# Modulation vectors of a diffusion block on VectorE: multiply-with-sum over transposed weights, streamed through attention

## What is computed

```python
for i in range(2):
    mx = silu(c) @ mod_w[i] + mod_b[i]                 # (6 * 1024,): shift, scale, gate, twice
    sh1, sc1, g1, sh2, sc2, g2 = split(mx, 6)
    h = rmsnorm(x, norm_mix_w[i]) * (1 + sc1) + sh1
    x = x + g1 * mixer_i(h)                            # i = 0: latent attention; i = 1: convolution
    h = rmsnorm(x, norm_ffn_w[i]) * (1 + sc2) + sh2
    x = x + g2 * (routed_experts(h) + shared_expert(h))
out = rmsnorm(x, final_norm_w)
```

## Time and profile before

| | |
|---|---|
| timed runs | 2271.82, 2284.52, 2284.88 us, median 2284.52 |
| profiled execution | 2278.05 us, span 2276.3 us |
| mean granted TensorE clock | 0.932 of full speed |
| DMA | 624 MB, 274 GB/s over the span |

### The profile page before, as it was taken

How to read it: one execution, slowest core, us unless ns; L and a number is a source line. 1 busy time by engine, 2 the same in 40 slices (tenths; PEclk the granted TensorE clock), 3 DMA queues, 4 the chain that set the end, 5 groups by cost and what they waited for, 6 DMA issues and landing times.

```text
span 2276.3 us, 30747 instructions
## 1 busy us (share of the span) xinstructions
PE 1920.7 (84%) x9400; PEld 990.8 (44%) x9401; DVE 829.5 (36%) x1481; ACT 463.6 (20%) x826; POOL 347.8 (15%) x538
## 2 busy tenths in 40 slices
PE   5999999899999888988991798688989889988952
PEld 2455555435444444444440343234444445444521
DVE  2126666504432222222225479425422222222226
ACT  4114444313011111111110355312111101111102
POOL 0000000000111111111105078101011111111122
PEclk8999999998999999999996799798999999999986
DMA  9589000368499999999986500016799999999954
GB/s 371 201 356 346 1 1 1 139 233 336 142 359 415 405 391 399 393 406 394 392 296 240 212 0 1 0 37 260 289 401 403 396 396 407 401 403 390 388 198 170
DMA packets 122815, 624.04 MB, mean 274 GB/s; under 512 B 18048, under 2 KB 19200, under 8 KB 87040
## 3 DMA queue, kind: packets, MB, share of 16 engines
q1 hardware_dynamic: 71776, 498.65, 55.5%
q0 software_dynamic: 26112, 79.72, 9.8%
q10 hardware_dynamic: 24864, 44.84, 5.5%
HBM read 562.34 MB, written 76.28 MB: 281 GB/s over the span
## 4 chain that ended last, share of the span: by engine, by line
PE 62%; DMA 19%; DVE 8%; issue 5%; ACT 3%; POOL 2%; SPq 0%; ACTq 0%; DVEq 0%; POOLq 0%
DMA ring<-in 17%; PE PS L942 10%; PE PS L936 10%; PE PS L1155 5%; PE PS L949 5%; PE PS L963 5%; PE PS L974 4%; PE PS L832 3%; PE PS L1172 3%; PE PS L927 2%; PE PS L861 2%; PE PS L794 2%; POOL work L509 2%; PE PS L917 2%; PE PS L785 2%
## 5 line engine op out<-in xcount | busy, mean ns | idle before, releaser
L942 PE MATMUL PS<-ring,work 128*64 128x256 f32 x3360 | 420.2, 407 | 113.0 <-issue 110.3
L942 PEld LDWEIGHTS PS<-ring,work 128*64 128x64 f32 x3360 | 249.4, 146 | 259.7 <-issue 165.6
L1308 DVE TENSOR_TENSOR work<-work,PS 64x256 f32<-64x256 f32 x105 | 44.4, 423 | 527.9 <-ACT work L583 524.6
L949 PE MATMUL PS<-ring,work 128*64 128x512 f32 x840 | 203.3, 605 | 1.4 <-ACT work L609 0.7
L936 PE MATMUL PS<-ring,work 128*128 128x512 f32 x400 | 177.5, 597 | 15.1 <-issue 12.3
L1313 DVE COPY work<-PS 128x1024 f32<-128x1024 f32 x128 | 156.8, 1225 | 14.7 <-PE PS L974 5.2
L461 POOL COPY col_i<-idx 128x1 int32 (+1 forms) x128 | 23.1, 181 | 839.8 <-PE PS L974 830.4
L467 POOL DMA_INDIRECT work<-h_rows,col_i x128 | 125.5, 981 | 169.0 <-issue 169.0
L974 PE MATMUL PS<-cst,work 128*128 128x128 f32 x1040 | 140.9, 278 | 0.5 <-DMA work<-h_rows,col_i 0.5
L583 ACT ACTIVATE work<-PS 64x256 f32<-64x256 f32 x105 | 39.4, 375 | 489.4 <-PE PS L942 489.4
L974 PEld LDWEIGHTS PS<-cst,work 128*128 128x128 f32 x1040 | 113.4, 141 | 54.0 <-issue 53.0
(11 more groups left out here) (226 smaller groups left out, 2228.5 us busy)
## 6 DMA issues: line engine op xcount, KB each, us to landing
ring<-in SPq DMA_DIRECT2D x156, 2048.0 KB, 11.1
ring<-in SPq DMA_DIRECT2D x130, 1024.0 KB, 12.0
y_rows<-zrow POOLq DMA_DIRECT2D x2, 14336.0 KB, 70.8
y_rows<-work ACTq DMA_DIRECT2D x210, 128.0 KB
ring<-in SPq DMA_DIRECT2D x3, 4096.0 KB, 27.2
y_rows<-work ACTq DMA_DIRECT2D x46, 256.0 KB
ring<-in SPq DMA_DIRECT2D x1, 8192.0 KB, 25.0
ring<-in SPq DMA_DIRECT2D x2, 3072.0 KB, 12.2
```

Of the source, the lines that this page charges most:

```text
L942: last = mm(bank(6)[64 * q:64 * q + 64, 0:F], lhs(c)[:, 0:64], w13(s)[:, q, c, :], start=(c == 0), stop=(c == DC - 1), tile_position=(0, 6 ...
L949: last = mm(bank(4)[64 * q:64 * q + 64, :], actT[par][:, kk, 0:64], w2(s)[:, kk, q * 512:(q + 1) * 512], start=(kk == 0), stop=(kk == 1), ...
```

## The change

- The four chunks that give shift and scale of layer 0's first sub-layer stay on TensorE. The other 10240 columns are computed on VectorE: their weights are transposed on the host, so that 128 of them lie on the partitions with 1024 inputs each, and a block (`mod_block`) is one multiply-with-sum of 128x1024 against SiLU of `c`, which is laid on all partitions by a broadcast load and one SiLU on ScalarE before its first square. Four blocks are a unit, one contiguous load of 2 MB. There are 20 units.
- Units 0 to 4 share one buffer of `ring`, at 12288: 0 and 1 stand on VectorE in front of the key part, 2 to 4 in front of the third latent norm. Units 5 to 13, 36 blocks, stand one block behind the transposes' copy of step n wherever 36n/64, rounded down, goes up. Units 14 to 19 stand three blocks behind each residual of the output projection. They alternate between two buffers at 16384 and 20480. Bias and gain follow in the middle of attention and behind the last block.
- `wq_b` and `wkv_b` are loaded as soon as chunks 0 and 1, and 2, are multiplied, before unit 0. `wo` goes to the start of `ring` and is loaded behind the last up-projection. Router and shared weights of layer 0 wait for the last block.
- The zeros are read from one row of 512 in DRAM instead of `zrow`.
- All weights lie as the SBUF holds them, one contiguous run for each partition. The semaphores of the experts' slots are shared by both layers.

```diff
@@ -42,6 +42,8 @@
+MOD_ROWS = (6 - 2 + 6) * DC
+UNITS = MOD_ROWS // 4
...
@@ -135,12 +137,14 @@
-        mrow = [work[:, n * 512:(n + 1) * 512] for n in range(12)]
+        mrow = [work[:, n * 512:(n + 1) * 512] for n in range(4)]
...
-        wo_sb = ring[:, AW:AW + DC * D].rearrange("p (c f) -> p c f", c=DC)
+        AT = (12288, AW, AW + 4096)
+        mod_tile = [ring[:, at:at + 4 * D].rearrange("p (j d) -> p j d", j=4) for at in AT]
+        wo_sb = ring[:, 0:DC * D].rearrange("p (c f) -> p c f", c=DC)
...
@@ -310,8 +316,17 @@
-        ROW_BANK = [n % 2 for n in range(4)] + [3, 0] * 4 + [(2, 4, 5, 6)[n % 4] for n in range(12)]
-        COL_BANK = [2] * 4 + [3] * 8 + [7] * 12
+        LOADS = [sum(slot_of(u) == n for u in range(E)) for n in range(RING)]
...
+        ROW_BANK = [n % 2 for n in range(4)]
+        COL_BANK = 2
+        EARLY = 5
...
+        ATTN_BLOCKS = 4 * (UNITS - 6 - EARLY)
...
+        def unit_home(u):
+            return (0, u + 1) if u < EARLY else (1 + (u - EARLY) % 2, (u - EARLY) // 2 + 1)
...
@@ -349,15 +363,19 @@
-                if n % 12 >= MODBUF:
-                    sp.wait_ge(modrow_ps, n - MODBUF + 1)
-                j = n % 12
-                sp.dma_start(mw[n % MODBUF], mod_w[n // 12, :, j * 512:(j + 1) * 512].rearrange("(c p) f -> p c f", p=128))\
-                  .then_inc(modw_in[n % MODBUF], 16)
+                sp.dma_start(ring[:, n * DC * 512:(n + 1) * DC * 512], mod_w[n]).then_inc(modw_in[n], 16)
...
+            def load_unit(u):
+                at, n = unit_home(u)
+                if u < EARLY:
+                    sp.wait_ge(modt_used, u)
+                elif u >= EARLY + 2:
+                    sp.wait_ge(modt_used, u - 1)
+                sp.dma_start(mod_tile[at].rearrange("p j d -> p (j d)"), mod_t[u]).then_inc(modt_in[at], 16)
...
-                sp.dma_start(rw_sb, router_w[i].rearrange("(c p) e -> p c e", p=128)).then_inc(rw_in, 16)
+                sp.dma_start(rw_sb.rearrange("p c e -> p (c e)"), router_w[i]).then_inc(rw_in, 16)
...
@@ -408,29 +426,30 @@
+            sp.dma_start(cs_row, c_row.partition_broadcast(128)).then_inc(crow_in, 16)
...
-            sp.dma_start(wqa_sb, wq_a.rearrange("(c p) f -> p c f", p=128)).then_inc(aw_in, 16)
-            sp.dma_start(wkva_sb, wkv_a.rearrange("(c p) f -> p c f", p=128)).then_inc(aw_in, 16)
-            for n in range(MODBUF, 12):
-                load_mod(n)
-            sp.wait_ge(modrow_ps, 12)
-            sp.dma_start(wqb_sb, wq_b.rearrange("(c p) (h f) -> p c h f", p=128, h=H)).then_inc(bw_in, 16)
-            sp.dma_start(wkvb_sb, wkv_b.rearrange("(c p) (h f) -> p c h f", p=128, h=H)).then_inc(bw_in, 16)
+            sp.dma_start(ring[:, AW:AW + DC * (QL + KVW)], w_a).then_inc(aw_in, 16)
+            sp.wait_ge(modrow_ps, 3)
+            sp.dma_start(ring[:, 0:8192], wq_b).then_inc(bw_in, 16)
+            sp.dma_start(ring[:, 8192:12288], wkv_b).then_inc(bw_in, 16)
+            sp.wait_ge(modrow_ps, 4)
+            for u in range(EARLY):
+                load_unit(u)
...
-            sp.dma_start(wo_sb, wo.rearrange("(c p) f -> p c f", p=128)).then_inc(wo_in, 16)
+            for u in range(EARLY, UNITS - 6):
+                load_unit(u)
...
-            for n in range(12, 15):
-                load_mod(n)
+            sp.dma_start(ring[:, 0:DC * D], wo).then_inc(wo_in, 16)
+            for u in range(UNITS - 6, UNITS):
+                load_unit(u)
...
-            for n in range(15, 24):
-                load_mod(n)
-            sp.wait_ge(wo_ps, DC)
+            sp.wait_ge(modt_used, UNITS)
...
-            sp.dma_start(pw1_sb, pw1.rearrange("(c p) f -> p c f", p=128)).then_inc(pw_in, 16)
-            sp.dma_start(pw2_sb, pw2.rearrange("(c p) f -> p c f", p=128)).then_inc(pw2_in, 16)
+            sp.dma_start(pw1_sb.rearrange("p c f -> p (c f)"), pw1).then_inc(pw_in, 16)
+            sp.dma_start(pw2_sb.rearrange("p c f -> p (c f)"), pw2).then_inc(pw2_in, 16)
...
@@ -514,7 +533,7 @@
-                               zrow[:, :].unsqueeze(1).to_broadcast([128, E // 2 + XMAX, 512])).then_inc(zero_out, 16)
+                               zero_d.unsqueeze(1).to_broadcast([128, E // 2 + XMAX, 512])).then_inc(zero_out, 16)
...
@@ -538,9 +557,12 @@
+            a.wait_ge(crow_in, 16)
+            A(cs_row, cs_row, ACT.Silu).then_inc(crow_rdy, 1)
...
-                A(mrow[n % 12], bank(ROW_BANK[n]), ACT.Copy).then_inc(modrow_sb, 1)
+                A(mrow[n], bank(ROW_BANK[n]), ACT.Copy).then_inc(modrow_sb, 1)
...
@@ -716,16 +736,11 @@
-            for n in range(DC + 1):
-                if n < DC:
-                    mod_row(12 + n)
-                if n:
-                    a.wait_ge(wo_ev, n)
-                    square(J_FFN0, n - 1)
+            for n in range(DC):
+                a.wait_ge(wo_ev, n + 1)
+                square(J_FFN0, n)
...
-            for n in range(20, 24):
-                mod_row(n)
...
@@ -831,8 +843,6 @@
-                for n in LATE[LSQ.index(g)] if g in LSQ else []:
-                    mod_chunk(n)
...
@@ -920,7 +926,6 @@
-                mod_chunk(12 + n)
...
@@ -1130,10 +1129,6 @@
-            for n in range(20, 24):
-                mod_chunk(n)
-            for n in range(12, 20):
-                mod_columns(n)
...
@@ -1205,6 +1199,31 @@
+            def mod_block(u, j):
+                at, n = unit_home(u)
+                g, c = u // 2, 4 * (u % 2) + j
+                i, part = (0, 2 + g) if g < 4 else (1, g - 4)
+                if j == 0:
+                    dve.wait_ge(modt_in[at], 16 * n)
+                last = V.scalar_tensor_tensor(mod_tile[at][:, j, :], mod_tile[at][:, j, :], 1.0, cs_row, ALU.mult, ALU.mult,
+                                              accum_out=mod[i][:, part, c, 0:1])
+                if j == 3:
+                    last.then_inc(modt_used, 1)
...
+            def mod_unit(u):
+                for j in range(4):
+                    mod_block(u, j)
...
+            def mod_done(i, units, p0, p1, gains):
+                dve.wait_ge(modt_used, units)
+                link(V.tensor_tensor(mod[i][:, p0:p1, :, 0].rearrange("p s c -> p (s c)"),
+                                     mod[i][:, p0:p1, :, 0].rearrange("p s c -> p (s c)"),
+                                     v("modb", 48 * i + DC * p0, 48 * i + DC * p1), ALU.add))
+                for n, g in gains:
+                    last = V.scalar_tensor_tensor(modA[i][:, n, :, 0], mod[i][:, 3 * n + 1, :, 0], 1.0,
+                                                  v(g, DC * i, DC * i + DC), ALU.add, ALU.mult)
+                last.then_inc(mod_rdy, 1)
...
@@ -1217,7 +1236,10 @@
-            mod_out(0, 4, COL_BANK[0], 0, 2, [(0, "nmix")])
+            mod_out(0, 4, COL_BANK, 0, 2, [(0, "nmix")])
+            dve.wait_ge(crow_rdy, 1)
+            mod_unit(0)
+            mod_unit(1)
...
@@ -1235,6 +1257,9 @@
+                if J == 2:
+                    for u in range(2, EARLY):
+                        mod_unit(u)
...
@@ -1256,7 +1281,6 @@
-            mod_out(0, 12, COL_BANK[4], 2, 6, [(1, "nffn")])
...
@@ -1284,12 +1308,18 @@
-            dve.wait_ge(mod_rdy, 2)
+                for b in range(n * ATTN_BLOCKS // NS, (n + 1) * ATTN_BLOCKS // NS):
+                    mod_block(EARLY + b // 4, b % 4)
+                if n == NS // 2:
+                    mod_done(0, 8, 2, 6, [(1, "nffn")])
...
+                for b in range(3 * n, 3 * n + 3):
+                    mod_block(UNITS - 6 + b // 4, b % 4)
+            mod_done(1, UNITS, 0, 6, [(0, "nmix"), (1, "nffn")])
...
@@ -1360,8 +1390,6 @@
-                if i == 0:
-                    mod_out(1, 24, COL_BANK[12], 0, 6, [(0, "nmix"), (1, "nffn")])
...
@@ -1606,8 +1634,13 @@
-    ins = [feats(a["x"][0]), feats(a["ctx"][0]), vec, constants(), a["mod_w"], a["mla_wq_a"][0], wq_b, wkv_a, wkv_b,
-           a["mla_wo"][0], a["conv_pw1_w"][0], a["conv_pw2_w"][0], a["router_w"], a["router_bias"], exp_w, sh_w]
+    w_a = np.concatenate([on_partitions(a["mla_wq_a"][0], DC), on_partitions(wkv_a, DC)], axis=1)
+    mod_w = np.stack([on_partitions(a["mod_w"][0][:, n * 512:(n + 1) * 512], DC) for n in range(4)])
+    mod_t = np.concatenate([a["mod_w"][0][:, 2 * D:], a["mod_w"][1]], axis=1).T
+    mod_t = mod_t.reshape(UNITS, 4, 128, D).transpose(0, 2, 1, 3).reshape(-1, 128, 4 * D)
+    ins = [feats(a["x"][0]), feats(a["ctx"][0]), vec, constants(), a["c"], np.zeros((1, 512), np.float32), mod_w, mod_t, w_a,
+           on_partitions(wq_b, QL // 128), on_partitions(wkv_b, KVL // 128), on_partitions(a["mla_wo"][0], DC),
+           on_partitions(a["conv_pw1_w"][0], DC), on_partitions(a["conv_pw2_w"][0], DC), on_partitions(a["router_w"], DC), a["router_bias"], exp_w, sh_w]
...
```

50 lines of the change are left out of this document (18 added, 32 removed).

## The result

The changed kernel took 2305.54 us, the median of eight runs (2294.7 to 2325.09); the kernel before, beside it on the same chip, 2283.6. The ratio is 1.0114, with a 95% interval of 1.0069 to 1.0158: slower, by about 1%. The eight times stand in two groups, 2294.7 to 2299.1 and 2312.0 to 2325.1, four in each, with a mean of 2297.4 and of 2318.6. The profiled execution, 2311.96 us, is of the upper one.

A forecast was written before the change was run, and what follows sets the result against it. TensorE, busy 84% of the span, was taken as the bound, so only what ends last counts. Terms +0.5 + 20.0 - 14.8 - 7.1 = -1.4 gave 2276.7 (profiled) or 2283.1 (median); forecast 2280 us, range 2252 to 2312.

The forecast's parts named there:

- Start: Before the down-projections: the broadcast of c and a SiLU delay ScalarE's first square, all serial; loss 2.4 us, bounds 1.0 to 6.
- Early loads: Units 0 to 4 before attention: each load beside the zeros takes 11 us, bounds 7.2 to 14.6; attention starts 0.5 later.
- That rival: Early unit loads starve beside zeros from one DRAM row: 20 us each, attention 28 later, 2308 us; chance 0.18.
- Restart at half clock: At attention's query half, TensorE restarts after some 20 us of idle at the 1.2 GHz level: a loss of 2.35 us.
- Attention: In attention, 36 blocks of 1.35 us on VectorE cost 20.0 us where its chain runs; bounds 0 to 49.
- My own table of steps: Cost of an attention block by step: 1.14 us behind 2, 1.35 behind 3 or 4, 0.64 behind 5 or 6, otherwise nothing.
- The rival of free blocks: VectorE's blocks cost nothing in attention because it idles 110 of 300 us: 2260 us, 2252 with quickest loads; chance 0.17.
- Output projection and norm: After attention, up to the score transposes: removed TensorE chunks gain 14.8 us in the projection and 7.1 in the norm.
- Contiguous weights: Weight loads: no wait of TensorE on them is on the chain; only early unit loads profit, experts' loads are unchanged.
- A sum kept halves the rate: Rival for all VectorE blocks: keeping the sum makes a block 2.4 us instead of 1.35, total 2321 us; chance 0.06.

The follow-up runs named there:

- e1: The changed kernel with the zeros read from a cleared SBUF row again, unit 6's load waiting for them: 2287.03 us, ratio 1.0009 to the kernel before.
- b2: The kernel before with only the zeros read from one 2 KB DRAM row: 2284.01 us beside 2282.94, ratio 0.9997.
- e4: The changed kernel with its 36 attention blocks moved to steps where VectorE waits: 2297.74 us, ratio 1.0052 to the kernel before.
- b3: The kernel before with convolution matrices laid out by partition, in two runs each (32 KB, 16 KB): 2284.67 us beside 2281.37, ratio 1.0023.
- f1: The changed kernel with the convolution matrices issued only after the last gathered row is added: 2299.24 us, ratio 1.0071 to the kernel before.
- b1: The kernel before with only the two convolution matrices made contiguous for each partition: 2296.3 us beside 2282.94, ratio 1.0038.

## Why the prediction was wrong

I predicted 2280 us and no change that can be measured; it is 2305.5 and slower. Two terms failed, both of transfers: the load of an early unit, taken as 11 us where it took 21, and the contiguous matrices, put at nothing. The terms of the engines held to 4 us.

**Start: too high.** Term +2.4. ScalarE's first square starts at 16.19 instead of 13.78, 2.41 later, as reckoned. But at the four modulation chunks TensorE is 1.8 late (36.05 against 34.28 on its timelines), and the columns behind them take 3.73 instead of 4.88, so what follows is only 0.6 late. I took the whole stretch as serial.

**Early loads: the step that failed.** I took 11 us for a unit's load beside the zeros, with 14.6 as its upper bound, from the output matrix beside zeros that came from SBUF. The loads measured 21. Unit 0 landed at 64.5 (65.6 reckoned), units 1, 3 and 4 at 90.5, 141.0 and 166.7 (82.4, 124.1 and 140.9 reckoned). I had let the load take turns with the zeros from its first packet on. The turns were about right, some 9 us for a unit (9.3 reckoned by turns of packets); the 11 us of zeros ahead of its first packet were not in the sum. The row came from another kind of transfer, and I used its rate although I had named the difference as a rival. That rival is what happened: a load of 20 us, attention 28 later (23 measured), 2308. I gave it 0.18. e1 and b2 show that it had the right cause, the source of the zeros. That its 2308 lies 2.5 us from the median is in part luck: attention cost less than summed, and in half of the executions the gather cost what no rival had. With zeros from SBUF, e1, the query projection started at 153.6 as I had summed (152.5), even though a load took 13.6 there and not 11: the blocks were shorter and the start earlier, so that slips cancelled.

**Restart at half clock: right.** The first 16 records of 512 columns took 9.24 against 6.88, a loss of 2.36; the term was 2.35.

**Attention: right, with a smaller block.** Predicted +20.0, measured +16.4. The blocks start every 1.15 us (the timeline gives each 1.22 and 0.08 for reading out the sum, and the next begins before the last has ended), and I had 1.35. My own table of steps with 1.15 gives 0.94, 1.15 and 0.44 for steps 2, 3 or 4, and 5 or 6: 16.5 for eight pairs of heads, 16.0 without the last pair's 0.44. So the step that failed is only the price of the unit. e4 shows the mechanism: the same blocks elsewhere cost nothing. The rival of free blocks was wrong for this placement.

**Output projection and norm: right.** From the first output column to the last xT 60.4 us instead of 74.8, -14.4 (reckoned -14.8); from there to the transposes 16.8 instead of 24.2, -7.4 (reckoned -7.1). The agreement is better than the measurement allows: the profiled execution of before has the shortest such stretch of its code. Its 64 records of line 775 took `536.68 8.89 PE PS L775 x64`, those of b3 `538.07 11.62 PE PS L775 x64`, at a mean granted clock of 0.86 and 0.75 from the last output column to the transposes. Against the 102.2 us of most kernels with the old code the change gains 25 here, not 22.

**Contiguous weights: the other step that failed.** "No wait of TensorE on any of them is on the chain" was true and not the question. What a load costs is also what it does to the transfers beside it. The trace of before had the gathers' times, and the matrices issued 2.3 us behind the last one. I looked at who waits for the matrices and not at who shares the queues with them. The price where the gather is hit is 17 us in the profiled stage (719.0 against 702.0 before and 701.5 in f1). By the times it falls on half of the executions of the changed kernel and on some eight of twelve of b1; there the groups' means lie 21 and 19 us apart.

**A sum kept halves the rate: wrong.** 80 blocks have a mean of 1218 ns, no more than the same shape without a kept sum. The rule of the Trainium skill (Vector Engine (DVE) Microarchitecture Reference, "Points that are easy to get wrong"), by which, as I read it, a block would be 2.4 us, does not hold for this instruction here.

**The sum again with what the runs showed:** +23.4 + 16.4 - 21.7 - 1.5 = +16.6 where the gather is not hit, 2300.2 from the median of before beside it; f1 measured 2299.24, 17.9 above its own before. Where it is hit, 17 more.

What stays open: why the copy from one DRAM row is slow. The runs show that each packet takes longer, and no more. No run reads the zeros from many DRAM rows, so whether the one row that all share makes it slow, or DRAM as the source, is untested. Open is also why some 20 packets of zeros on each engine pass ahead of a unit's first, and what in an execution decides whether the last gather is hit at an issue distance of 1.7 to 1.9 us.

## What to carry to other kernels

Price a transfer from a row with the same source, destination and run length, or call its price unknown and keep the far end in the range; and for each load whose shape changes ask which small transfers stand in the queues beside it, not only who waits for it. A load issued beside a large copy pays twice, for what passes ahead of its first packet and for the turns behind it. Work moved onto an engine with idle time costs by its place, so put it ahead of that engine's long waits: the same 36 blocks were worth 16 us or nothing. When the times of a kernel stand in two groups, compare group with group, and force the cause one way by an issue moved earlier or later before its size is read.

## What the hardware showed that I had not expected

- 28.7 MB written from one 2 KB row in DRAM landed after 192 to 216 us in every kernel that had them so, from a row in SBUF after 69 to 82 us. While only these ran, the queues moved 90 to 136 GB/s in the changed kernel.
- A 2 MB load issued beside these zeros had its first packet after 11 to 12 us (4 to 5 with zeros from SBUF, 1 without zeros), and was then through in some 9 (8 and 7).
- A gather of 128 rows of 4 KB, 6 us by itself, takes 9.9, 16.1 and 26.9 us beside a load whose runs are 8, 32 and 64 KB. A load of long runs is hardly faster for it here: the first matrix took 23.1 to 25.4 us in runs of 64 KB, and 24.6 to 27.9 in runs of 8 KB.
- A multiply with kept sum of 128x1024 float32 in SBUF takes 1.22 us and repeats every 1.15; one of the same shape without it, in the combination, takes 1.29. The sum's read-out, 0.08 us, hides in that.
